# Weights' buffers moved on by 32 bytes inside their partitions

## The reference

```
f = (silu(norm(x) @ w_gate) * (norm(x) @ w_up)) @ w_down      # 1024 -> 2 x 2816 -> 1024, six times
x = x + 0.5 * norm(f)                                         # plain sum, without norm, in e and f
q, k, v = norm(x) @ w                                         # and the like in conv, attn, even, odd
```

## Time and profile before

| | |
|---|---|
| median of 3 runs | 1678.07 us (1676.02 to 1678.69) |
| the profiled execution | 1674.97 us, its span 1673.6 us |
| TensorE busy | 1629.4 us, 97% of the span, 7938 matmuls |
| VectorE busy | 973.9 us, 58% |
| ScalarE busy | 787.4 us, 47% |
| DMA engines' share | 46.6% (weight queue) |
| granted TensorE clock | 0.996 of full speed |

### The profile page before, as it was taken

One profiled execution on the slowest core, in us unless ns is written; L12 is line 12 of the kernel. 1 busy time (PEld: TensorE's weight loads), 2 busy tenths in 40 slices (PEclk: granted clock), 3 DMA queues, 4 the chain that ended last, 5 costly groups with the idle time before them and its releaser, 6 DMA issues.

```text
span 1673.6 us, 18645 instructions
## 1 busy us (share of the span) xinstructions
PE 1629.4 (97%) x7938; PEld 1333.0 (80%) x7938; DVE 973.9 (58%) x1004; ACT 787.4 (47%) x957; POOL 69.5 (4%) x99
## 2 busy tenths in 40 slices
PE   6999999999999999998999999999999999899999
PEld 5877876888888888797888888977788887578887
DVE  4654676645456545646554556878645457855453
ACT  4534454544344434445543445745534345744342
POOL 1000000100001000100100000010000002000000
PEclk9999998999999999999999999999999999999999
DMA  8545452455445545452554555442455444245451
GB/s 326 189 174 184 169 187 101 149 219 186 183 171 204 199 175 200 165 207 101 208 194 176 195 182 189 152 139 67 160 216 192 175 172 179 76 145 189 178 194 50
DMA packets 51392, 289.33 MB, mean 173 GB/s; under 512 B 14152, under 2 KB 14792, under 8 KB 18027
## 3 DMA queue, kind: packets, MB, share of 16 engines
q1 hardware_dynamic: 50732, 286.84, 46.6%
q10 hardware_dynamic: 576, 1.29, 0.2%
HBM read 287.06 MB, written 1.05 MB: 172 GB/s over the span
## 4 chain that ended last, share of the span: by engine, by line
PE 90%; DVE 6%; ACT 3%; issue 1%; POOL 1%; DMA 0%; SPq 0%; DVEq 0%; ACTq 0%
PE ps L529 86%; PE ps L628 2%; PE ps L538 1%; DVE wl L1939 1%; ACT wh L1263 1%; ACT scg L1852 0%; DMA gains<-in_rows 0%; PE ps L1140 0%; DVE tmp L1970 0%; DVE x L1972 0%; DVE scg L2638 0%; DVE xc L2448 0%; POOL st L2712 0%; DVE smn L2451 0%; POOL st L2709 0%
## 5 line engine op out<-in xcount | busy, mean ns | idle before, releaser
L1939 DVE TENSOR_TENSOR wl<-raw,wh 128x2048 fp32r<-128x2048 f32 x260 | 588.6, 2287 | 154.4 <-ACT wh L1263 154.4
L529 PE MATMUL ps<-wh,xTh 128*128 128x512 f32 x1408 | 558.1, 396 | 9.1 <-DVE wl L1939 5.3
L529 PE MATMUL ps<-wh,xTl 128*128 128x512 f32 x1408 | 551.1, 391 | 0.0
L529 PE MATMUL ps<-wl,xTh 128*128 128x512 f32 x1408 | 550.4, 391 | 0.0
L1263 ACT ACTIVATE wh<-raw 128x2048 fp32r<-128x2048 f32 x260 | 488.5, 1908 | 3.5 <-PE ps L529 2.2
L529 PEld LDWEIGHTS ps<-wh,xTh 128*128 128x128 f32 x1408 | 265.6, 189 | 73.6 <-issue 11.5
L529 PEld LDWEIGHTS ps<-wh,xTl 128*128 128x128 f32 x1408 | 265.4, 188 | 56.3
L529 PEld LDWEIGHTS ps<-wl,xTh 128*128 128x128 f32 x1408 | 265.8, 189 | 53.0
L2709 POOL TENSOR_SCALAR st<-st 128x1 f32<-128x1 f32 (+2 forms) x46 | 28.9, 628 | 1417.1 <-ACT tmp L1282 830.8
L1326 ACT ACTIVATE sgf<-ps,st 128x256 f32<-128x256 f32 x22 | 10.4, 474 | 104.1 <-PE ps L529 104.1
L1326 ACT ACTIVATE sge<-ps,st 128x256 f32<-128x256 f32 x22 | 10.4, 473 | 97.6 <-PE ps L529 97.6
(11 more groups left out here) (334 smaller groups left out, 2251.7 us busy)
## 6 DMA issues: line engine op xcount, KB each, us to landing
raw<-in_w SPq DMA_DIRECT2D x260, 1024.0 KB, 4.8
gains<-in_rows SPq DMA_DIRECT2D x18, 512.0 KB, 3.9
x<-in_x ACTq DMA_DIRECT2D x2, 512.0 KB, 7.9
nab<-in_rpb SPq DMA_DIRECT2D x32, 32.0 KB, 2.5
out_x<-x SPq DMA_DIRECT2D x2, 512.0 KB, 2.6
nabfirst<-in_rpb SPq DMA_DIRECT2D x16, 32.0 KB, 2.8
qn<-in_rpb SPq DMA_DIRECT2D x16, 32.0 KB, 2.5
df<-in_cst SPq DMA_DIRECT2D x1, 368.0 KB, 23.4
```

The lines of the kernel that those rows point to most:

```text
L529: return pe.matmul(o, lhs, rhs, start=start, stop=stop, skip_group_check=False)
L1939: TT(wl[:, p % RAW, :], raw[:, p % RAW, :], wh[:, p % RING, :].bitcast(F32), ALU.subtract).then_inc(*lo(p))
```

## The change

An unused buffer of eight float32 columns (32 bytes) is declared ahead of `raw`, and another behind `wh`. The first moves `raw`, `wl` and `wh` on by 32 bytes, to bytes 1184 and 58528: they go from 0 to 32. Everything behind the second has moved by 64 bytes in all, and keeps its remainder. No instruction is added, removed or reordered, and no wait is changed.

```diff
@@ -282,10 +282,12 @@
         def bank(b, n=1):
             return ps[:, 512 * b:512 * (b + n)]
 
+        sb("gap0", [128, 8])
         with ExitStack() as same:
             raw = sb("raw", [128, RAW, 2048], F32, same)
         wl = sb("wl", [128, RAW, 2048], F32R)
         wh = sb("wh", [128, RING, 2048], F32R)
+        sb("gap1", [128, 8])
         x = sb("x", [128, 2, D])
         xTh = sb("xTh", [128, 8, 2, 128], F32R)
         xTl = sb("xTl", [128, 8, 2, 128], F32R)
```

## The result

The changed kernel takes 1691.28 us, the median of 4 runs (1691.1 to 1692.01), against 1678.05 us for the kernel before (4 runs). The ratio is 1.0082, with an interval from 1.0066 to 1.0098: 13.2 us slower. Its profiled execution took 1691.1 us with a span of 1689.7 us, 16.1 us more than the 1673.6 us of before.

What follows compares the result with a forecast made beforehand. TensorE, busy 97% of the span, was taken as the bound, through the start-to-start time of matmuls. 26.8 - 11.1 - 0.7 = +15.0 us took the profiled execution to 1690.0 us, the median to 1693.1; range 1676 to 1707 us.

Steps and rivals of the forecast that it cites:

- Both signs inside it: Streaming weights against xTh/xTl get slower, +26.8 us; streaming weights against hT and oT get faster, -11.1 us.
- The reading of before: 512-column matmuls of the kernel before: 226.8 ns when both operands lie alike, 6.8 ns more when they differ by 32 bytes.
- The rival without a beat at 32: The beat may need both operands at 0, so down gains nothing: +26 us, 1704 us; chance 0.18.
- that of each operand for itself: Each operand at 32 costs by itself, so down loses 11.1 us: 1715 us; chance 0.07.
- that of cheap streaming: Streaming at 32 is as cheap at 512 columns as at 256, project -7.2 us: 1659 us; chance 0.13.
- only the loaded operand counts or that nothing does: 512-column matmuls keep their steps, project_t moves by -1 to +4 us: about 1678 us; chance 0.10.
- Item 1: 4224 project matmuls, weights against xTh/xTl, go from alike to differing: 6.8 ns in feed-forward layers, 5 elsewhere, +26.8 us.
- Item 2: 1632 down matmuls, weights against hT and oT, go from differing to both at 32: -6.8 ns each, -11.1 us.
- Item 3: project_t, 256 columns: 576 matmuls become unlike, -1.0 us, and 192 become alike, +0.3 us; together -0.7 us.
- Items 4 and 5: VectorE's and ScalarE's splits stay as they are; weight loads 0 to +2 us, taken as 0.
- The chain piece forecast at 16.65 us: TensorE's unbroken piece of 72 matmuls in stages b to f: 16.65 us instead of 16.48.
- I count them in full: Almost all affected matmuls lie in TensorE's unbroken pieces, so their changes count fully, with no new wait.

Runs made afterwards that it cites:

- experiment 1: Kernel before with one unused 32-byte buffer behind mhalf, so hT, oT, q move from 32 to 0 like the weights: 1670.38 us against 1675.66, ratio 0.9965.
- experiment 2: Kernel before with unused 32-byte buffers ahead of raw and behind mhalf, so weights, xT, hT, oT and q all lie at 32: 1670.77 us, ratio 0.9967.
- experiment 5: Two kernels: the one before with xT moved to 32, hT staying there, 1697.46 us; the changed one with hT, oT, q moved to 0, 1696.99 us.
- experiment 4: The changed kernel's two unused buffers made 64 bytes instead of 32, weights moved by 64 and the rest by 128: 1695.41 us, ratio 1.0118 to the kernel before.
- experiment 3: Kernel before with 32-byte buffers between wl and wh and behind wh, so wh alone moves to 32, raw and wl stay at 0: 1688.09 us, ratio 1.0072.
- experiment 10: Kernel before with hTh and hTl of each feed-forward layer at different distances from the weights (b 0 and 32, f 64 and 0): 1673.81 us, one run.

## Why the prediction was right, and where it was not

The forecast was 1693.1 us for the median, 1.8 us above the measured 1691.28, and 1690.0 us for the profiled execution, 1.1 us below its 1691.1. Both signs inside it came as forecast.

*The reading of before*, that the 6.8 ns belong to two operands lying unlike, held: experiments 1 and 2 put them alike at two absolute places and `down` falls to 226.4 ns both times; experiment 5 puts them equally unlike at two places and both take 1697 us. The rival without a beat at 32 (1704 us) and that of each operand for itself (1715 us) are refuted by experiment 2, that of cheap streaming (1659 us) by 4224 matmuls at 233.2 ns. The same 233.2 ns refute that only the loaded operand counts or that nothing does, for `xT` kept its remainder.

*Item 1* was +26.8 us and measured +24.9 as mean times count (+23.5 in the paired steps): 5.9 ns on average instead of 6.8 and 5.

*Item 2* is the term that was mis-sized: -11.1 us, measured 1632 x -4.1 = -6.7 (-5.4 in the paired steps). The step that failed is giving all 1632 matmuls the full 6.8 ns because the beat would be "found at once after a `project` run". Behind a `project` run it is (227.1 ns), but more than half of the `down` matmuls stand behind the transposes, and there it is not (230.0 ns). That is a run-in which the earlier trace rows had shown for conv and which I didn't apply here. And layer a doesn't get the beat at all: after the change it lies 128 bytes from the weights, 232.3 ns. That is the second fault under the same item. I counted remainders modulo 64, and the earlier trace rows don't tell 64 from 256; experiment 4, 17 us off my expectation, did.

*Item 3* was -0.7 and measured -1.5: the streaming runs went to 117.4 rather than 118.4 ns. Two rows of it, `project_t` in even and in attn:
```profile
1048.36 0.28 PE L531 MATMUL ps<-xTh,wl 128*128 128x256 f32 x1
...
1076.12 0.28 PE L531 MATMUL ps<-xTl,wh 128*128 128x256 f32 x1
```
```profile
763.97 0.28 PE L531 MATMUL ps<-qh,wl 128*128 128x256 f32 x1
...
775.24 0.28 PE L531 MATMUL ps<-ql,wh 128*128 128x256 f32 x1
```
The first is 27.76 us over 238 steps, 116.6 ns, against 120.1 in the earlier trace rows. The second is 11.27 us over 94 steps, 119.9 ns: it is alike now and slower than the earlier trace rows.

*Items 4 and 5* held: in the page's groups the splits have the same means, and a piece of weights lands in the same 4.8 us as in the earlier trace rows.
```profile
L1941 DVE TENSOR_TENSOR wl<-raw,wh 128x2048 fp32r<-128x2048 f32 x260 | 588.6, 2287 | 154.5 <-ACT wh L1265 154.5
...
L1265 ACT ACTIVATE wh<-raw 128x2048 fp32r<-128x2048 f32 x260 | 488.4, 1908 | 3.6 <-PE ps L531 2.3
...
raw<-in_w SPq DMA_DIRECT2D x260, 1024.0 KB, 4.8
```
The chain piece forecast at 16.65 us measured 16.68 to 16.70 in b to f: 48 x 233.2 + 12 x 227.1 + 12 x 230.0 = 16.68 us.

The total is closer than its terms, and that is luck. As mean times count, item 1 was 1.9 us too high, item 2 took off 4.4 us too much and item 3 0.8 us too little, which leaves the sum of the steps 1.7 us too low. A term that the prediction put at nothing goes the other way: "I count them in full" overlooks that gaps in which TensorE waits take up some of the slower matmuls, 2.2 us here and 3.5 us in experiment 4. At a like clock +16.4 and -2.2 give +14.2 us, where the medians differ by 13.2. For the profiled execution the forecast also kept the clock of before, 0.996; the run had 0.992, which gave back about what the waits had taken.

The Trainium skill's rule (TensorE: Matmul & The Clock Gate, Step-by-step), that loading the next weights takes no read bandwidth from the running matmul, doesn't hold as a rule of no interaction: moving the one operand against the other moves the repeat from 226.7 to 233.3 ns here (experiments 2 and 5). The line of 16 bytes (the Trainium skill, SBUF — State Buffer, Specifications) doesn't set the price either: 16, 32, 64 and 128 bytes are all multiples of it, and behind a `project` run one is free while three are not.

Open: what the two reads share, for no run looks inside them and a conflict of two reads is my reading, not shown; why the price hardly grows from 32 bytes to 224; what decides which of the three matmuls pays (experiments 3 and 10); and about 1 us between the paired steps and waits and the medians.

## What to carry to other kernels

When TensorE is the bound and each matmul comes with its own load, read the start-to-start distance and not the length of a record, and compare products by their addresses. Here, for 512 streaming columns of float32r, put the operand that is loaded at the same place modulo 256 bytes as the one that streams; one unused buffer of 32 bytes gave 0.35% (experiment 1). Move all operands that stream in turn together: with `wh` and `wl` unlike, the table doesn't hold (experiment 3). Count a gain like this only for matmuls in unbroken runs, expect waits elsewhere to take up part of a change, compare runs at a like granted clock, and test a period that was inferred from two places with a third place before building on it.

## What was not expected

- The distance counts modulo 256 bytes: 0 and 256 give 227 ns, 32, 64, 96, 128, 160 and 224 about 233. 16 is like 0 behind a `project` run (226.7 ns) and like 32 behind the transposes (232.6).
- At 256 streaming columns the sign is the other way round: on average alike 120.0 to 120.5 ns, unlike 116.6 to 118.3.
- Behind a break even operands that lie alike need time to fall into step: by position, the first ten `down` distances behind the transposes were 229, 232, 235, 227, 232, 233, 228, 229, 229 and 227 ns in the changed kernel (b to f), where operands that lie unlike have 232.7 on average. The `project` runs of the kernel before show the same behind gaps of more than 260 ns: 232 ns in the first three distances, 229 to 230 in the next three, 227 to 228 from the tenth on.
- An unused buffer of 32 bytes in a partition, in the right place, is worth 5.3 us here (experiment 1); two of them in the places of the change cost 13.2.
